# First up blocks of the second layer's gated MLP: two blocks' first halves interleaved tile by tile

## What is computed

```python
mix = einsum('bthe,hed->btd', o, diff_w_out)          # attention output projection
x = x + gt1[:, None, :] * mix                         # gated residual
h = modulate(rms_norm(x, norm_ffn[i]), sh2, sc2)      # h * (1 + scale) + shift
up = einsum('btd,de->bte', h, w_in)                   # first step of conv_ffn
conv = conv_b + sum(conv_w[j] * padded[:, j:j + T])
u, gate = split(conv, 2); y = einsum('btf,fd->btd', silu(gate) * u, w_out)
```

## Time and profile before

| | |
|---|---|
| median of 3 runs | 1384.91 us (1384.88 to 1385.6) |
| the profiled execution's own time | 1384.99 us |
| its span, first to last instruction | 1383.2 us |
| PE busy | 1371.2 us, 99% of the span |
| DVE, ACT, POOL busy | 69%, 48%, 7% |
| share of PE in the chain that ended last | 95% |
| mean granted TensorE clock | 0.998 of full |

### The profile page before, as it was taken

One profiled execution on the slowest core, in us unless ns is written; L12 is line 12 of the kernel. 1 busy time (PEld: TensorE's weight loads), 2 busy tenths in 40 slices (PEclk: granted clock), 3 DMA queues, 4 the chain that ended last, 5 costly groups with the idle time before them and its releaser, 6 DMA issues.

```text
span 1383.2 us, 26341 instructions
## 1 busy us (share of the span) xinstructions
PE 1371.2 (99%) x10882; PEld 1295.3 (94%) x10882; DVE 949.3 (69%) x1595; ACT 659.4 (48%) x1467; POOL 92.3 (7%) x152
## 2 busy tenths in 40 slices
PE   9999999999999999999999999999999999999999
PEld 6888888999999999999988888889899999999999
DVE  5688677479888788688765746576897653554554
ACT  5543434466553354252565655645665542552520
POOL 0000000200000000000400000001200000000000
PEclk9999999999999999999999999999999999999999
DMA  9644542344444544535333323113244223223222
GB/s 379 242 172 147 181 150 84 102 149 132 161 145 165 179 160 131 178 121 193 115 150 107 127 92 122 64 63 123 92 138 138 84 69 96 88 73 112 77 75 100
DMA packets 38015, 182.43 MB, mean 132 GB/s; under 512 B 4294, under 2 KB 6854, under 8 KB 26632
## 3 DMA queue, kind: packets, MB, share of 16 engines
q1 hardware_dynamic: 22984, 126.98, 26.5%
q0 software_dynamic: 14912, 53.78, 11.2%
HBM read 172.82 MB, written 7.91 MB: 131 GB/s over the span
## 4 chain that ended last, share of the span: by engine, by line
PE 95%; DVE 2%; ACT 1%; DMA 1%; issue 1%; POOL 0%; SPq 0%; DVEq 0%; POOLq 0%; ACTq 0%
PE ps L669 28%; PE ps L671 27%; PE ps L670 27%; PE ps L1079 2%; PE ps L1129 1%; PE ps L1038 1%; PE ps L1101 1%; PE ps L928 1%; PE ps L924 1%; PE ps L915 1%; PE ps L707 1%; PE ps L759 1%; DMA xT<-in_xT 0%; PE ps L1122 0%; DMA w_raw<-in_wst 0%
## 5 line engine op out<-in xcount | busy, mean ns | idle before, releaser
L671 PE MATMUL ps<-h_hi,w_lo 128*128 128x272 f32 x2048 | 592.9, 289 | 0.0
L669 PE MATMUL ps<-h_hi,w_hi 128*128 128x272 f32 x1952 | 568.9, 291 | 3.2 <-DVE h_lo L1787 2.7
L670 PE MATMUL ps<-h_lo,w_hi 128*128 128x272 f32 x1952 | 561.9, 288 | 0.0
L671 PEld LDWEIGHTS ps<-h_hi,w_lo 128*128 128x128 f32 x2048 | 385.5, 188 | 0.0
L669 PEld LDWEIGHTS ps<-h_hi,w_hi 128*128 128x128 f32 x1952 | 368.1, 189 | 11.6 <-issue 6.0
L670 PEld LDWEIGHTS ps<-h_lo,w_hi 128*128 128x128 f32 x1952 | 368.6, 189 | 1.0 <-issue 1.0
L1191 ACT CAST w_hi<-w_raw 128x2048 fp32r<-128x2048 f32 (+2 forms) x106 | 179.1, 1691 | 195.2 <-PE ps L671 168.2
L1702 DVE TENSOR_TENSOR w_lo<-w_raw,w_hi 128x2048 fp32r<-128x2048 f32 (+2 forms) x105 | 214.9, 2046 | 63.7 <-ACT w_hi L1191 63.1
L670 PE MATMUL ps<-act_lo,w_hi 128*128 128x272 f32 (+1 forms) x704 | 203.7, 289 | 0.0
L669 PE MATMUL ps<-act_hi,w_hi 128*128 128x272 f32 (+1 forms) x704 | 203.6, 289 | 0.1
L671 PE MATMUL ps<-act_hi,w_lo 128*128 128x272 f32 (+1 forms) x704 | 203.1, 288 | 0.0
(11 more groups left out here) (284 smaller groups left out, 1774.2 us busy)
## 6 DMA issues: line engine op xcount, KB each, us to landing
w_raw<-in_wst SPq DMA_DIRECT2D x72, 1024.0 KB, 4.8
a_raw<-in_ada_r POOLq DMA_DIRECT2D x56, 512.5 KB, 4.1
w_raw<-in_wst SPq DMA_DIRECT2D x28, 768.0 KB, 4.3
a_raw<-in_ada_g POOLq DMA_DIRECT2D x24, 512.0 KB, 3.5
a_pro<-in_ada_p SPq DMA_DIRECT2D x8, 1024.0 KB, 16.5
v_raw<-in_wst SPq DMA_DIRECT2D x8, 1024.0 KB, 8.1
w_raw<-in_wst SPq DMA_DIRECT2D x10, 512.0 KB, 5.9
xT<-in_xT SPq DMA_DIRECT2D x4, 544.0 KB, 5.2
```

The source lines that it names most:

```text
L669: mm(out, lhs_hi, rhs_hi, start=first, stop=False)
L670: mm(out, lhs_hi, rhs_lo, start=False, stop=False)
L671: return mm(out, lhs_lo, rhs_hi, start=False, stop=last)
```

## The change

PE gets `last_pair` for b1 and b2 of layer 1; `first_pair` stays for the other passages. In the first half b2 follows b1 tile by tile, four tiles behind. stats(3, 1) moves from behind b1's seventh tile to behind b1's eighth and b2's fourth; b2's last four tiles follow it. The second halves are as before. b2's weights are wanted from b1's fourth tile on, so ACT's two half splits of b2 move up among the first half's squares, and DVE's `low` of b2 is cut into two halves, one ahead of half_tiles(3, 0, (0,)) and one behind tile 3. DVE adds the last two units of DOUT_B to xT behind tile 4 and not behind tile 1, and ACT's last two squares move behind the shift of tile 5.

```diff
+PAIR_LAG = 4
+            def last_pair(name):
+                us = pair_units(name)
+                n = BN[name]
+
+                def tile(pair, k):
+                    for u in pair:
+                        ins = three(*unit_terms(u, k), k == 0, k == KT - 1)
+                        if k == KT - 1:
+                            ins.then_inc(unit_done, 1)
+
+                pe.wait_ge(w_lo_ok, n + 1)
+                for u in us[0:2]:
+                    bank_free(u)
+                for k in range(KT):
+                    pe.wait_ge(h_ok, H_BASE[4] + k + 1)
+                    tile(us[0:2], k)
+                    if k == PAIR_LAG - 1:
+                        pe.wait_ge(w_lo_ok, n + 2)
+                        for u in us[2:4]:
+                            bank_free(u)
+                    if k >= PAIR_LAG:
+                        tile(us[2:4], k - PAIR_LAG)
+                stats(3, 1)
+                for k in range(KT - PAIR_LAG, KT):
+                    tile(us[2:4], k)
+                for u in us[4:6]:
+                    bank_free(u)
+                for k in range(KT):
+                    pe.wait_ge(h_ok, H_BASE[4] + KT + k + 1)
+                    tile(us[4:6], k)
+                units(us[6:8])
@@ TensorE, ffn
-                        if name in PAIR_OF and kind == "up":
-                            first_pair(1 + 2 * l, name)
+                        if name in PAIR_OF and kind == "up" and l:
+                            last_pair(name)
+                        elif name in PAIR_OF and kind == "up":
+                            first_pair(1, name)
@@ ScalarE
-            for m in range(KT):
+            for m in range(4):
                 square(3, m, 0)
+            split(BN[("up", 1, 0, 1)], 0)
+            square(3, 4, 0)
+            square(3, 5, 0)
+            split(BN[("up", 1, 0, 1)], 1)
+            square(3, 6, 0)
+            square(3, 7, 0)
             for m in range(3):
                 square(3, m, 1)
             half_root(3, 0)
...
             square(3, 4, 1)
             square(3, 5, 1)
-            half_modulated(3, 0, (2,))
+            half_modulated(3, 0, (2, 3, 4, 5))
             square(3, 6, 1)
             square(3, 7, 1)
-            half_modulated(3, 0, (3,))
-            split(BN[("up", 1, 0, 1)], 0)
-            half_modulated(3, 0, (4, 5))
-            split(BN[("up", 1, 0, 1)], 1)
-            half_modulated(3, 0, range(6, KT))
+            half_modulated(3, 0, (6, 7))
             half_root(3, 1)
@@ VectorE
             last_out(DOUT_B[KT:KT + 4])
+            low(BN[("up", 1, 0, 1)], 0)
             half_tiles(3, 0, (0,))
             last_out(DOUT_B[KT + 4:KT + 6])
-            half_tiles(3, 0, (1,))
+            half_tiles(3, 0, (1, 2, 3))
+            low(BN[("up", 1, 0, 1)], 1)
+            half_tiles(3, 0, (4,))
             last_out(DOUT_B[KT + 6:])
-            half_tiles(3, 0, range(2, KT))
-            low(BN[("up", 1, 0, 1)])
+            half_tiles(3, 0, (5, 6, 7))
             half_tiles(3, 1, range(KT))
```

## The result

The changed kernel takes 1388.58 us (median of 11 runs, 1388.47 to 1389.19) against 1385.12 us for the kernel before on the same chip (11 runs, 1384.49 to 1386.14): a ratio of 1.0025, 95% interval 1.0017 to 1.0033, or 3.46 us more. The forecast was 1389.0, slower by 4.1. The profiled execution took 1388.47 us itself, with a span of 1386.7.

A forecast was written before the change was run, and what follows sets the result against it. The prediction took PE as the bound, with the chain behind stats(3, 1) ending the passage: the statistic 4.6 us later, less 0.6 of cover, added 4.1 to 1384.99, median 1389.0 us; range 1386.8 to 1390.9.

The forecast's parts named there:

- What bounds, and what ends the passage: Behind stats(3, 1): a chain through ACT and DVE lies open, ending b1's second half 13.1 us after the statistic starts.
- The splits hidden: ACT's two half splits of b2 lie in its waits for POOL, cost nothing; stats(3, 0) stays at 970.2.
- Half of `low`: DVE's first half of `low` ahead of tile 0 takes 1.2 us and makes scaling 1.0 us late.
- Tiles 2 to 4: b1's first half: h_lo ready at 979.5, 980.5 and 982.45; PE waits 1.1 us for tile 4.
- The price of the low clock: b1's tiles 2 to 6 in the kernel before: half clock cost 1.4 us; not in the forecast sum.
- the 4.4 us that filling could give back: Passage of the kernel before: low clock 1.4 us plus idle stretches of 1.47 and 1.55, the most filling could return.
- the rival at 1390.4: Clock falls again in tiles 4 to 7 (1.4 us) or the second half (0.5): 1390.4; 14 in 100.
- Tile 5: b1's first half: POOL's last addition meets this tile's h_lo, ready at 984.85; PE waits 0.8 us.
- The waits of the second half: b1's second half: PE waits 0.3 to 0.5 us for h_lo at each tile, about 3.5 in all.
- Without a wait: First halves: h_lo comes as fast as PE takes it, stats(3, 1) at 984.0, time 1383.4; 4 in 100.
- The splits' cover: Rival: ACT's splits are not covered, stats(3, 0) and all behind it move by 0.5 to 1: 1389.8; 6 in 100.

The follow-up runs named there:

- the kernel with the statistic last: The kernel before with stats(3, 1) alone moved behind all of b2's first half: 1391.89 us, ratio 1.0049.
- the kernel with the statistic between b2's units: The kernel before with stats(3, 1) alone moved between the two units of b2's first half: 1389.51 us, ratio 1.003.
- stats earlier: The changed kernel with stats(3, 1) alone moved to behind b1's tile 6: 1386.75 us, ratio 1.001.
- `low` in the gap: The changed kernel with the first half of b2's `low` made ahead of adding unit DOUT_B[11]: 1389.13 us, ratio 1.0026.
- no lag: Against the changed kernel: b2 right behind b1 tile by tile, stats(3, 1) behind tile 3, DVE and ACT orders changed: 1385.55 us, ratio 0.9997 to the kernel before.
- the two kernels with one tile of lag in the first halves only: Against the changed kernel: b2 one tile behind b1, stats(3, 1) behind tile 3, ACT and DVE reordered: 1383.3 us; the same with DOUT_B[11] added first: 1383.16.
- the root first: The changed kernel with half of `low` ahead of DOUT_B[11] and ACT's first-half root ahead of the third square: 1387.69 us, ratio 1.0019.

## Why the prediction came out right, and the term that was mis-sized

**What bounds, and what ends the passage.** Shown. The chain behind stats(3, 1) was forecast as 13.1 us to the end of b1's second half and came as 1002.03 − 988.87 = 13.16. In the eight kernels where ACT and DVE were ready for it, the last h_lo ended 12.25 or 12.26 us after stats(3, 1) started, at starts from 984.87 to 992.75.

**The splits hidden.** Right. ACT's two halves of b2's split stand at 965.97 and 967.94, and stats(3, 0) at 970.34 against 970.23.

**Half of `low`.** Right: 1.22 us where 1.2 was taken. Tile 0 was forecast for 975.85 and came at 975.79; tile 1 for 978.25 and came at 978.09.

**Tiles 2 to 4.** h_lo ended at 979.37, 980.32 and 982.28 against 979.5, 980.5 and 982.45. The clock fell once and tile 4's wait swallowed it, as forecast: PE worked at 1.2 GHz through 978.4 to 981.8, and had 0.17 us of idle time left ahead of tile 4 where the forecast had 1.1 at full clock.

**The price of the low clock.** Wrong, though it isn't in the sum. The prediction took 5.23 − 3.76 us and called it the clock's cost of 1.4. But DVE brings a tile only every 0.95 us there. In the kernel with the statistic last, whose clock was full in that stretch, tiles 2 to 6 took 979.92 to 984.72, which is 4.80 us, so the clock cost the kernel before 0.4 us there. Its executions agree: on the chips of the experiments those at a mean granted clock of 1.000 have a median 0.3 to 0.4 us below the others. So the 4.4 us that filling could give back were about 3.4, and the rival at 1390.4 was priced too high for the first halves. In the second half, where it had 0.5, the one run whose clock fell there lost nothing at the end. In the changed kernel the fall cost nothing that its executions show: the five at 1.000 took 1388.47 to 1389.19, the six at 0.999 took 1388.47 to 1388.66, which is what the forecast meant by the waits swallowing it.

**Tile 5: the term that was mis-sized.** I put POOL's last addition on the h_lo of tile 5 and had it ready at 984.85. That addition started at 983.36 and took 1.43 us, and what it held was the scaling of tile 7, 0.88 us instead of 0.50. h_lo of tile 5 took 0.50 and ended at 984.17. From there PE ran as forecast, so stats(3, 1) came at 988.87 and not at 989.5. That is the 0.6 us between 4.1 and 3.46.

**The waits of the second half.** Right in size, read by starts: a tile every 1.2 us (995.48, and the next two at 996.68 and 997.89) for 0.75 us of work, so 0.45 a tile. As idle time the profile shows only 0.2 of each.

**The rivals.** "Without a wait" fell: tiles 0 to 3 had nothing beside them. It took a lag of one tile, another order on DVE and on ACT, and an earlier statistic to get below the kernel before. The clock fell only once in the changed kernel's profile. The splits' cover held.

**Open.** Why the clock falls in one execution of a kernel and not in the next isn't settled; no run varied PE's idle time alone. Nor did a run vary the lag alone, with all other orders kept.

## What to carry to other kernels

A statistic that starts a chain over other engines (reduce, root, scale, split) has a due time: its consumer's start less the chain, here 12.25 us. Before interleaving two blocks, count the matmuls that still stand behind the statistic; if they take less time than the chain, move the statistic first, which here gave back 2.0 of 3.5 us for one moved call. Look also for what else the old place of the statistic covered: here it hid the wait for b2's `low`. Move work on a vector engine only after reading who shares its port and what stands behind that engine's partner in the next queue.

## What the runs showed of the hardware that was not expected

The fall of the granted clock is not the same from execution to execution, of one and the same kernel. Of the kernel before, 20 of the 33 executions on one chip have a mean granted clock of 1.000 and 8 have 0.998; of the kernel with the statistic between b2's units, 3 of 7 have 1.000 and 4 have 0.998. So a profile shows one draw: 3.4 us at half clock in those of the kernel before, of the changed one and of three experiments (stats earlier, `low` in the gap, no lag), and 6.8 us in the two with the statistic late. It is not chance alone, for all 22 executions of the two kernels with one tile of lag in the first halves only have 1.000. In the profile with the root first (8 of its 11 executions have 1.000) the clock did not fall, with PE idle for 1.19 us ahead of 977.31 and for 1.03 ahead of 981.65. The windows of that profile show PE at work for 3.50 of 5 us and then 3.90 of 5, at full clock:

```profile
975.00:980.00 5.00, 3.50 (x24) 2.91 (x24) 4.93 (x11) 2.41 (x6) 2.29 (x3) 1.00 0.63 210
980.00:985.00 5.00, 3.90 (x29) 3.50 (x29) 4.79 (x12) 2.41 (x5) 2.42 (x3) 1.00 0.00 0
```

An addition of POOL, 0.77 us by itself, took 1.75 to 1.83 us in all seven kernels with `low` in the gap, where a DVE subtraction of 1.22 us had begun just before it. The other way round, in the kernel with the statistic earlier, that subtraction began at 973.16 while POOL added until 973.52, and took 1.44. Neither engine shows the delay as a wait; it stands in the duration of the instruction.
